# A head norm's inverse root: from square root and VectorE reciprocal to logarithm and exponential on ScalarE

## What is computed

```python
def diff_attn(q, k, v, lam):
    s = jnp.einsum('bhqd,bhkd->bhqk', q, k) * (HEAD_DIM ** -0.5)
    a = jax.nn.softmax(s, axis=-1).reshape(b, N_HEADS, 2, nq, nk)
    w = a[:, :, 0] - lam * a[:, :, 1]
    return jnp.einsum('bhqk,bhkd->bhqd', w, v)

def head_out(o, g_sub, lam_init):          # the head norm
    o = rms_norm(o, g_sub) * (1.0 - lam_init)
    ...
def rms_norm(x, g):
    return x * lax.rsqrt(jnp.mean(x * x, axis=-1, keepdims=True) + EPS) * g
```

## Time and profile before

| | before |
|---|---|
| median of 3 runs | 3588.51 us (3586.37 to 3588.83) |
| profiled execution | 3586.86 us, its span 3585.5 us |
| mean granted TensorE clock | 0.98 |
| PE busy | 3408.4 us (95%) |
| DVE busy | 1323.7 us (37%) |
| ACT busy | 800.8 us (22%) |
| POOL busy | 1578.2 us (44%) |

### The profile page before, as it was taken

How to read it: one execution, slowest core, us unless ns; L and a number is a source line. 1 busy time by engine, 2 the same in 40 slices (tenths; PEclk the granted TensorE clock), 3 DMA queues, 4 the chain that set the end, 5 groups by cost and what they waited for, 6 DMA issues and landing times.

```text
span 3585.5 us, 42527 instructions
## 1 busy us (share of the span) xinstructions
PE 3408.4 (95%) x17440; PEld 2687.4 (75%) x17452; DVE 1323.7 (37%) x2282; ACT 800.8 (22%) x1608; POOL 1578.2 (44%) x996
## 2 busy tenths in 40 slices
PE   6989999999999999999999898889999989889998
PEld 4667777788866677777778787778888878667886
DVE  5843313311159333132122665641211255551113
ACT  2243411100022444111011334320110123420111
POOL 3413356566544134664565421233333333235664
PEclk8999999999999999999999999999999999999999
DMA  6434122333233441335442210132432311114321
GB/s 203 135 127 143 48 90 94 106 94 94 84 99 124 130 130 48 94 103 161 130 141 83 81 48 24 37 106 71 141 118 95 106 51 59 36 47 138 97 94 59
DMA packets 403370, 346.80 MB, mean 97 GB/s; under 512 B 9701, under 2 KB 400613, under 8 KB 403178
## 3 DMA queue, kind: packets, MB, share of 16 engines
q1 hardware_dynamic: 395328, 336.62, 30.0%
q10 hardware_dynamic: 7850, 7.47, 0.7%
HBM read 341.96 MB, written 2.10 MB: 96 GB/s over the span
## 4 chain that ended last, share of the span: by engine, by line
PE 88%; DVE 6%; ACT 3%; issue 1%; DMA 1%; POOL 1%; ACTq 0%; DVEq 0%; POOLq 0%
PE psum L575 26%; PE psum L577 25%; PE psum L576 25%; PE psum L557 2%; PE psum L837 2%; PE psum L983 1%; PE psum L954 1%; PE psum L825 1%; PE psum L769 1%; DVE psum L1838 1%; PE psum L665 1%; DVE k L2358 1%; PE psum L812 1%; PE psum L810 1%; PE psum L814 1%
## 5 line engine op out<-in xcount | busy, mean ns | idle before, releaser
L515 POOL TENSOR_SCALAR weights_hi<-raw_weights 128x1024 fp32r<-128x1024 f32 (+3 forms) x496 | 498.0, 1004 | 1937.1 <-PE psum L577 1617.7
L575 PE MATMUL psum<-h_hi,weights_hi 128*128 128x512 f32 (+1 forms) x2832 | 1139.5, 402 | 70.0 <-DVE h_lo L1880 54.2
L518 POOL TENSOR_TENSOR weights_lo<-raw_weights,weights_hi 128x1024 fp32r<-128x1024 f32 (+3 forms) x496 | 1089.0, 2196 | 41.4
L577 PE MATMUL psum<-h_hi,weights_lo 128*128 128x512 f32 (+1 forms) x2832 | 1077.8, 381 | 0.0
L576 PE MATMUL psum<-h_lo,weights_hi 128*128 128x512 f32 (+1 forms) x2832 | 1076.3, 380 | 0.0
L575 PEld LDWEIGHTS psum<-h_hi,weights_hi 128*128 128x128 f32 x2832 | 538.8, 190 | 230.7 <-issue 111.1
L576 PEld LDWEIGHTS psum<-h_lo,weights_hi 128*128 128x128 f32 x2832 | 538.9, 190 | 117.1 <-issue 15.6
L577 PEld LDWEIGHTS psum<-h_hi,weights_lo 128*128 128x128 f32 x2832 | 537.9, 190 | 109.0
L575 PE MATMUL psum<-hidden_hi,weights_hi 128*128 128x512 f32 (+1 forms) x1120 | 411.7, 368 | 0.0
L576 PE MATMUL psum<-hidden_lo,weights_hi 128*128 128x512 f32 (+1 forms) x1120 | 411.3, 367 | 0.0
L577 PE MATMUL psum<-hidden_hi,weights_lo 128*128 128x512 f32 (+1 forms) x1120 | 410.8, 367 | 0.0
(11 more groups left out here) (284 smaller groups left out, 3599.3 us busy)
## 6 DMA issues: line engine op xcount, KB each, us to landing
raw_weights<-in_ada_w SPq DMA_DIRECT2D x96, 1024.0 KB, 5.3
raw_weights<-in_w_mlp SPq DMA_DIRECT2D x64, 1024.0 KB, 5.2
raw_weights<-in_w_in SPq DMA_DIRECT2D x54, 1024.0 KB, 5.4
raw_weights<-in_w_ffn_in SPq DMA_DIRECT2D x88, 512.0 KB, 5.2
raw_weights<-in_w_out SPq DMA_DIRECT2D x16, 1024.0 KB, 5.0
raw_weights<-in_w_ffn_out SPq DMA_DIRECT2D x16, 1024.0 KB, 5.0
raw_weights<-in_w_in SPq DMA_DIRECT2D x30, 512.0 KB, 4.2
raw_weights<-in_w_branch SPq DMA_DIRECT2D x56, 128.0 KB, 2.2
```

What stands on the lines that cost most here:

```text
L515: gpsimd.tensor_scalar(whi[:, r, c0:c1], raw[:, raw_slot, c0:c1], 1.0, 1.0, ALU.mult, ALU.mult).then_inc(*split_hi.up(*key, half))
L518: gpsimd.tensor_tensor(wlo[:, r, c0:c1], raw[:, raw_slot, c0:c1], whi[:, r, c0:c1].bitcast(F32), ALU.subtract).then_inc(*split.up(*key, half))
L575: tensor.matmul(out, sh, mh, start=first, stop=False, skip_group_check=shared)
L577: return tensor.matmul(out, sl, mh, start=False, stop=last, skip_group_check=shared)
```

## The change

The mean of the context's squares goes to bank 7 instead of bank 6, and both means are made in the same step, context first; one semaphore step tells ScalarE that both are there. ScalarE takes, instead of a square root, the logarithm of both (context, then tokens) and, after waiting for them, one exponential of minus half of it over all 768 (layer 1: 512) columns. VectorE's reciprocal goes; it waits for the exponential and scales. The next head's values wait for bank 7 until the context's logarithm is done.

```diff
 (TensorE)
             def head_norm(n):
-                for s, (c0, c1) in reversed(list(enumerate(segs))):
-                    tensor.wait_ge(*squared.at(L, "head", n))
-                    tensor.wait_ge(*free[6])
-                    tensor.matmul(bank[6][:, 0:c1 - c0], meanm, k_t[:, n, c0:c1], start=True,
-                                  stop=True).then_inc(*meaned.up(L, "head", n, s))
-                    free[6] = rooted.at(L, "head", n, s)
-                    yield
+                tensor.wait_ge(*squared.at(L, "head", n))
+                for s, (c0, c1) in enumerate(segs):
+                    bk = 6 if c0 else 7
+                    tensor.wait_ge(*free[bk])
+                    ins = tensor.matmul(bank[bk][:, 0:c1 - c0], meanm, k_t[:, n, c0:c1], start=True, stop=True)
+                    free[bk] = rooted.at(L, "head", n, c0)
+                ins.then_inc(*meaned.up(L, "head", n))
+                yield
 (ScalarE)
             def head_norm(n):
-                for s, (c0, c1) in reversed(list(enumerate(segs))):
-                    scalar.wait_ge(*meaned.at(L, "head", n, s))
-                    scalar.activation(k_t[:, n, c0:c1], bank[6][:, 0:c1 - c0], ACT.Sqrt, bias=eps[:, 0:1],
-                                      scale=float(D // P)).then_inc(*rooted.up(L, "head", n, s))
-                    yield
+                x0 = TC if last else 0
+                scalar.wait_ge(*meaned.at(L, "head", n))
+                for c0, c1 in segs:
+                    scalar.activation(k_t[:, n, c0:c1], bank[6 if c0 else 7][:, 0:c1 - c0], ACT.Ln, bias=eps[:, 0:1],
+                                      scale=float(D // P)).then_inc(*rooted.up(L, "head", n, c0))
+                scalar.wait_ge(*rooted.at(L, "head", n, TC))
+                scalar.activation(k_t[:, n, x0:TA], k_t[:, n, x0:TA], ACT.Exp,
+                                  scale=-0.5).then_inc(*act_misc.up(L, "head", n))
+                yield
 (VectorE)
             def head_norm(n):
                 ho, rms = q_t[:, n, x0:TA], k_t[:, n, x0:TA]
-                vector.wait_ge(*rooted.at(L, "head", n, 0))
-                vector.reciprocal(rms, rms).then_inc(*inverted.up(L, "head", n))
-                vector.wait_ge(*inverted.at(L, "head", n))
+                vector.wait_ge(*act_misc.at(L, "head", n))
                 vector.scalar_tensor_tensor(out=ho, in0=ho, scalar=lams[:, 6:7], in1=rms, op0=ALU.mult,
                                             op1=ALU.mult).then_inc(*scaled.up(L, "head", n))
```

## The result

The changed kernel takes 3569.87 us (median of 5 runs, 3567.62 to 3570.07) against 3587.93 us for the kernel before beside it: a ratio of 0.9950, with a 95% interval of 0.9939 to 0.9961. That is 18.1 us less, where 22.9 were forecast. It lies inside the stated range (3559 to 3577), on the side of rival (a).

A forecast was written before the change was run, and what follows sets the result against it. TensorE, busy 95%, bounds the kernel; its waits near the heads hang on VectorE's reciprocal. Layer 0 -13.0, layer 1 -10.4, norms +0.5 give -22.9 us: 3565.6 by the median, stated as 3566, range 3559 to 3577.

The forecast's parts named there:

- rival (a): Only PE's direct waits go; layer 1's clock drop and follow-on waits remain: -16.9 us, 3571.6; chance 0.20 with shades toward no change.
- Heads 0 and 1 of layer 0: PE's waits for softmax exponential, rotation and values go, bank 6 costs 0.4 us more each: -2.7 and -4.7 us.
- heads 0 to 2 of layer 1: Waits for values or the pool branch shrink or go, half clock partly returns in head 0: -6.3, -3.0, -1.1 us.
- half of the stretch at half clock: Layer 1, head 0: shortening PE's wait also returns half of the 5.54 us run at clock 0.50, 2.8 us.
- head 2 of layer 0: The next maximum starts 5.6 us earlier, so -5.6 us; the splitting of outputs on DVE and ACT binds next.
- The work from there to PE's next wait is the same: Layer 0, head 2: work behind the earlier maximum was taken as unchanged, so the full 5.6 us count.
- the clock's 3.0 us turn into a wait: Layer 0, head 2: the 3.0 us lost at half clock become a new PE wait near the pool matmul.
- 8 + 8 + 1 + 2 loads: ScalarE table loads: 8 before logarithms, 8 before new exponentials, 1 at layer 1's start, 2 at norms; 19 instead of 21.
- Rival (b): No loads between logarithm and exponentials, softmax exponential 2.5 us earlier in six heads: about -7.6 us more, 3558; chance 0.07.
- Bank 6 in layer 0: PE's wait for bank 6 grows by 0.4 us in each of three heads, from 2.6 to 3.8 us.
- Rival (c): ScalarE's queue takes the reciprocal's place, load and exponential delaying the copy in each head: +13.8 us, 3602; chance 0.03.
- The norms: The two norms after the attention each gain a table load before the root: +0.4 us layer 0, +0.1 layer 1.

The follow-up runs named there:

- the regrouping alone: The changed kernel's order (both means together, context in bank 7) with square root and VectorE's reciprocal kept, no new exponential: 3588.94 us, ratio 1.0006 to the kernel before.

## Why the prediction was right, and where it was off

**What bounds the kernel: right.** PE's waits near the heads were set by the reciprocal one or two steps up the chain. With it kept, no regrouping and no saved load moved the time; with it put back at one head, the wait of that head came back.

**Right by head, five of six.** Heads 0 and 1 of layer 0 (-2.76 and -4.70 against -2.7 and -4.7), heads 0 to 2 of layer 1 (-6.41, -3.20, -1.27 against -6.3, -3.0, -1.1). The step that carried head 0 of layer 1, that half of the stretch at half clock is part of the wait's price, was confirmed by putting the reciprocal back: 6.5 us. Rival (a), which kept that stretch, has nearly the measured time by luck.

**Off: head 2 of layer 0, -5.6 forecast, -1.25 measured.** The step that failed is the sentence "The work from there to PE's next wait is the same". The maximum did come 5.86 us earlier, but the work behind it wasn't the same: it now lay under GpSimd's burst. Three operations took 7.10 us instead of 2.65, and these 4.45 us are what is missing. The rows of before had the sign of it: in that head's scaling, 1.97 us where 1.02 is usual, whose mean of 1.255 I put down to "slow ones" and read no further. It was shown from two sides, by giving the reciprocal back (+1.25) and by moving the burst (-4.51 by the ruler). A second part of that sentence's sum failed with it: "the clock's 3.0 us turn into a wait". In the changed kernel the half clock stayed (0.53 over 4.91 us of work) and the wait of 3 us forecast at the pool matmul wasn't there (0.6, as before). Both came as forecast once the burst was moved (clock 1.00, wait 2.51, head gain 5.76).

**ScalarE: right in count, a little off in time.** 8 + 8 + 1 + 2 loads, as forecast; ACT busy rose by 0.8 us instead of 3.4. By form the loads (2.6 us less) and the new exponentials (5.9 us more) are as forecast, and the single instructions' times add up to 3.1 us more (866.0 against 862.9). Busy time counts an overlap once, and an instruction that follows another without a load begins some 0.1 us before the other's end (the copy at 2226.39 behind an exponential that ends at 2226.49), which happens more often now; that this makes up the whole difference is an inference. Rival (b), no load between logarithm and exponential, fell: there are 8 loads at L1681. The Trainium skill (page "ScalarE: Activation LUTs", section "Table sets: the hidden batching unit") says that one set holds both functions, so that a logarithm and then an exponential need one load. These traces don't agree: every logarithm followed by an exponential, in the head norms and at the block's entry, has a load of 1.283 us between.

**The waits it added: right.** Bank 6 in layer 0, 3 x 1.23 us against 3.8 forecast; 0.3 for the scores of head 2 against 0.5. Rival (c) had no more than that.

**The norms: +0.4 and +0.1 forecast, +0.62 and +0.64 measured.** The load itself is worth 0.42 in layer 0 (the reciprocal starts 6.94 us earlier where the square ahead was 7.36) and 0.2 in layer 1. The other 0.2 of layer 0 lie within the scatter of that row. In layer 1 the clock differs too: over 13 us from the norm's root (from 3186.50 after, 3204.00 before) it was 0.61 after and 0.74 before; that this is the rest is not shown.

**The total.** -22.9 forecast; +4.35 for the burst and +0.76 for the norms, less 0.54 for small terms of the other heads, gives the measured -18.3 of the two traces. Range and signs held; rival (a)'s time was nearly met, its mechanism not.

## What to carry to other kernels

Shortening an operation of one engine moves what stands behind it, and it may land under another engine's burst: before counting a shift in full, look at what the other engines do in the stretch that the work moves into, and at single operations whose time is above the mean of their form. A split that isn't needed for tens of us can be held back by one semaphore wait (here 3.3 to 4.6 us for one line). And a reciprocal of a root on the path is dear (3.35 us for 512 columns): with a logarithm instead of the root, a load and an exponential on ScalarE cost 1.28 + 0.6 in its place, and this pays where PE stands still, which in this kernel were the wide norms most of all (15 us more).

## What the runs showed of the hardware

- Some VectorE operations on operands in SBUF take 1.6 to 4.2 times as long while GpSimd works through a split: 1.67 instead of 1.02 us, 3.09 instead of 0.95 (all 768 columns, as the next two), 2.98 instead of 1.02, 2.34 instead of 0.68, 2.89 instead of 0.69 (512 columns). The reciprocal (4.95 us with the burst on it, 4.95 without in head 1) and the maximum out of PSUM (1.75) aren't slowed. The three of head 2 end 0.41, 0.80 and 0.82 us after the end of the GpSimd instruction under which they began (2235.50, 2236.82, 2239.82), which is near what each takes alone (0.68, 1.02, 0.95), as if they stood still until it is through. GpSimd is held up in turn: in the kernel before L515 took 1.75 us beside the scaling and 1.04 beside the reciprocal, and L518, 2.34 us there, took 2.92 in the changed kernel beside the combine. The Trainium skill (page "SBUF — State Buffer", section "Who interferes with whom") states that VectorE and GpSimd share one pair of ports under an exclusive lock. By it a VectorE operation with two inputs in SBUF contends with a GpSimd instruction that reads SBUF, and so does one in a two-port mode, which tensor_scalar can enter; one with a single SBUF input outside those modes doesn't. The trace agrees on both kinds: scaling, combine and split were slowed, the reciprocal (4.95) and the maximum out of PSUM (1.75) weren't. The forecast didn't weigh it.
- PE waits of 4.1 to 4.2 us in head 0 of layer 1 were followed by half clock in all three kernels that had them (before, the old norm put back there, and the regrouping alone: 6.8, 6.8 and 3.4 us of it), and the wait of 0.9 us in the changed kernel by none. After waits of 1.9 us it came in some kernels and not in others, with the same waits ahead (0.84 and 1.00 granted over the same stretch of head 1 in two of them), and cost some 1.6 us each time. Single differences below 2 us between kernels with edits elsewhere shouldn't be read from one trace without a look at the clock.
- Six table loads fewer on ScalarE (7.7 us) were worth nothing where the loads lay in the engine's idle time.
